# A Trainium2 decoder kernel: context tiles first in two rotary chunks, the query scale moved into a copy, and branch rows turned one branch at a time

## The reference

```
h  = norm(x)                                  # 4 tiles of 128 rows: 0,1 tokens; 2,3 context
ka, va, kc, vc, qa, qc, zb = h @ w_in          # 512 columns each (zb: 1024)
ka, qa = rope_axial(ka), rope_axial(qa)        # token tiles only
ya = differential_attention(qa * 0.125, ka, va)
yb = spatial_gate(gelu(zb))
yc = neighbourhood_attention(qc * 0.125, kc, vc)
merged = sum over b of sigmoid(h @ w_gate[b]) * (y[b] @ w_branch[b])
x  = x + gate * (merged @ w_out);  then a routed mixture of 32 experts
```

## Time and profile before

| what | value |
|---|---|
| time of three runs, us | 3181.65, 3183.58 (median), 3187.3 |
| the profiled execution, its time / its span, us | 3185.1 / 3183.4 |
| mean granted TensorE clock, share of full | 0.951 |
| PE busy | 2817.2 us, 88% of the span |
| DVE / ACT / POOL busy | 1311.8 (41%) / 930.7 (29%) / 1044.3 (33%) |
| bytes moved | 746.03 MB, mean 234 GB/s |

### The profile page before, as it was taken

One profiled execution on the slowest core, in us unless ns is written; L12 is line 12 of the kernel. 1 busy time (PEld: TensorE's weight loads), 2 busy tenths in 40 slices (PEclk: granted clock), 3 DMA queues, 4 the chain that ended last, 5 costly groups with the idle time before them and its releaser, 6 DMA issues. The chain is left out here.

```text
span 3183.4 us, 33959 instructions
## 1 busy us (share of the span) xinstructions
PE 2817.2 (88%) x13329; PEld 1876.5 (59%) x13329; DVE 1311.8 (41%) x2392; ACT 930.7 (29%) x1303; POOL 1044.3 (33%) x431
## 2 busy tenths in 40 slices
PE   7999959999998798799987999998597897999885
PEld 4777638887776486577875444443485775433331
DVE  5552123334523426763345333322527545332223
ACT  0433313335333313441212222222324332222211
POOL 0277528742875244043420000000363671000000
PEclk9999979999999899999988999999799998999998
DMA  5755675555556432222233999999242456999996
GB/s 179 265 181 177 246 280 177 181 169 179 182 186 237 161 103 81 81 92 75 100 119 142 383 421 422 422 422 402 106 137 75 146 206 273 411 422 422 422 422 266
DMA packets 208913, 746.03 MB, mean 234 GB/s; under 512 B 13877, under 2 KB 15075, under 8 KB 158833
## 3 DMA queue, kind: packets, MB, share of 16 engines
q1 hardware_dynamic: 189872, 669.61, 55.5%
q0 software_dynamic: 18880, 74.22, 6.8%
HBM read 721.00 MB, written 44.27 MB: 240 GB/s over the span
## 5 line engine op out<-in xcount | busy, mean ns | idle before, releaser
L1886 POOL TENSOR_TENSOR weight_ring_r<-weight_ring,weights_high_r 128x2048 fp32r<-128x2048 f32 x136 | 622.7, 4589 | 460.2 <-ACT weights_high_r L1495 370.0
L1495 ACT ACTIVATE weights_high_r<-weight_ring 128x2048 fp32r<-128x2048 f32 x136 | 257.1, 1901 | 654.2 <-PE banks L848 415.4
L843 PE MATMUL banks<-weights_high_r,x_transposed_r 128*128 128x512 f32 x1008 | 400.9, 398 | 32.6 <-DVE scaled_rows L2663 11.4
L2011 POOL DMA_DIRECT2D moe_y<-arena x64 | 34.1, 533 | 925.7 <-DVE arena L2711 925.7
L848 PE MATMUL banks<-weight_ring_r,x_transposed_r 128*128 128x512 f32 x1328 | 323.9, 390 | 1.0 <-POOL weight_ring_r L1886 1.0
L1886 POOL TENSOR_TENSOR weight_ring_r<-weight_ring,gates_r 128x2048 fp32r<-128x2048 f32 (+1 forms) x60 | 270.7, 4524 | 156.2 <-DVE small L2053 96.1
L848 PEld LDWEIGHTS banks<-weight_ring_r,x_transposed_r 128*128 128x128 f32 x1328 | 250.0, 188 | 53.4 <-POOL weight_ring_r L1886 1.4
L843 PEld LDWEIGHTS banks<-weights_high_r,x_transposed_r 128*128 128x128 f32 x1008 | 192.3, 191 | 77.4 <-issue 21.4
L1736 ACT ACTIVATE arena<-banks 64x1024 f32<-64x1024 f32 x64 | 65.1, 1018 | 488.8 <-PE banks L1237 488.8
L844 PE MATMUL banks<-weights_high_r,arena_r 128*128 128x512 f32 x520 | 206.7, 397 | 0.0
L2696 DVE TENSOR_TENSOR arena<-banks,arena 64x1024 f32<-64x1024 f32 x64 | 78.2, 1222 | 295.2 <-ACT arena L1736 295.2
(11 more groups left out here) (394 smaller groups left out, 4744.8 us busy)
## 6 DMA issues: line engine op xcount, KB each, us to landing
weight_ring<-in_moe_w_up SPq DMA_DIRECT2D x64, 1024.0 KB, 19.3
x_transposed<-in_moe_w_up SPq DMA_DIRECT2D x60, 1024.0 KB, 19.0
tokens_out<-in_moe_w_down SPq DMA_DIRECT2D x60, 1024.0 KB, 17.3
arena<-in_moe_w_gate SPq DMA_DIRECT2D x60, 1024.0 KB, 19.1
weight_ring<-in_moe_w_down SPq DMA_DIRECT2D x60, 1024.0 KB, 17.6
weight_ring<-in_w_in SPq DMA_DIRECT2D x56, 1024.0 KB, 5.2
weights_high<-in_moe_w_gate SPq DMA_DIRECT2D x56, 1024.0 KB, 18.7
weight_ring<-in_ffn_w_in SPq DMA_DIRECT2D x44, 1024.0 KB, 5.3
```

The costliest lines, as they stand in the source:

```text
L843: nc.tensor.matmul(banks[t][:, 0:width], xh, wh[:, k, :], start=k0 + k == 0, stop=False)
L1495: nc.scalar.activation(high(s, kn, width), slot(c, kn, width), ACT.Copy).then_inc(high_ready, 1)
L1886: nc.gpsimd.tensor_tensor(slot(c, kn, width, ring_r), slot(c, kn, width), high(s, kn, width), ALU.subtract).then_inc(low_ready, 1)
L2011: nc.gpsimd.dma_start(ys_dram[e * CAP:(e + 1) * CAP, :], A[own(e), E_Y:E_Y + D]).then_inc(ys_out[e % 2], 16)
```

## The change

Four edits. (1) `tile_order` makes PE's last (low) products, the transposes and DVE's work go through the tiles as 2, 3, 0, 1 in chunk 0 of both `g_kv` and in chunk 2 of layer 0's `g_qz`. Banks are given out in that order too. The chunk after takes them in the order 0, 1, 2, 3, so its tile 0 gets the bank of the chunk's tile 2. (2) The scale 0.125 leaves `rope_axial` and stands in the copy of the turned query rows. (3) `gate_ahead` gets a step between its two halves: PE turns the rows of the first branch there. (4) The other two branches are turned behind the gate products of n = 0 and n = 1, DVE's `parts` are split in the same way, and PE waits for one branch's copies instead of all. `src_ready` is said once.

```diff
+        def tile_order(g, n):
+            if g in g_kv and n == 0 or g is g_qz[0] and n == 2:
+                return (2, 3, 0, 1)
+            return range(g.tiles)
...
-                for t in range(g.tiles):
+                for t in order:
                     if k0 == 0:
-                        banks.append(acc_bank())
+                        banks[t] = acc_bank()
...
-                banks = [acc_bank() for _ in range(g.tiles)]
+                order = tile_order(g, 0)
+                banks = {t: acc_bank() for t in order}
...
-            def gate_ahead(g, lhs, layer):
+            def gate_ahead(g, lhs, layer, between):
...
+                between()
                 pe.wait_ge(low_back, 16 * (layer + 1))
...
-                gate_ahead(g_gate[i][0], x_late, i)
-                for t in range(tiles):
-                    for b in range(3):
-                        pe.wait_ge(src_ready, seen.next(src_ready))
-                        transposes([ar(BRANCH[b] + t * 512 + j * P, P) for j in range(4)])
-                copied()
+                branch_turned = []
+
+                def turn_branch():
+                    for t in range(tiles):
+                        transposes([ar(BRANCH[len(branch_turned)] + t * 512 + j * P, P) for j in range(4)])
+                    branch_turned.append(made.now(tr_ready))
+
+                def first_branch():
+                    pe.wait_ge(src_ready, seen.next(src_ready))
+                    turn_branch()
+                gate_ahead(g_gate[i][0], x_late, i, first_branch)
                 for n in range(6):
                     b = n % 3
                     if n > 0:
                         product(g_gate[i][n], x_late)
+                    if n < 2:
+                        turn_branch()
+                    pe.wait_ge(tr_used, branch_turned[b])
...
-                if scale == 1.0:
-                    v(tt(dst, t1, turned, ALU.add), acc_used)
-                else:
-                    v(tt(t1, t1, turned, ALU.add))
-                    v(ts(dst, t1, scale, None, ALU.mult), acc_used)
+                v(tt(dst, t1, turned, ALU.add), acc_used)
...
-                    for t in range(MAX_TILES):
+                    for t in tile_order(g_kv[layer], n):
...
-                        for t in range(tiles):
-                            copy_turned(qaT[:, :, t * P:(t + 1) * P])
+                        for t in tile_order(g_qz[layer], 2):
+                            bank = turned_bank()[:, :].rearrange("p (k c) -> p k c", k=4)
+                            v(ts(qaT[:, :, t * P:(t + 1) * P], bank, 0.125, None, ALU.mult), tr_used)
...
-                say_n = 3 * tiles
-                for _ in range(say_n):
-                    say(src_ready)
+                say(src_ready)
+
+                def branch_parts(k):
+                    for t in range(tiles):
...
+                branch_parts(0)
                 for n in range(6):
...
+                    if n < 2:
+                        branch_parts(n + 1)
```

More of the change, by code:

```diff
@@ L832, in copied, with group @@
                 pe.wait_ge(tr_used, made.now(tr_ready))
-            def group(g, lhs, banks, c, s, k0, kn, width):
+            def group(g, lhs, banks, c, s, k0, kn, width, order):
                 pe.wait_ge(high_ready, s + 1)
                 wh, wl = high(s, kn, width), slot(c, kn, width, ring_r)
-                for t in range(g.tiles):
+                for t in order:
                     if k0 == 0:
-                        banks.append(acc_bank())
+                        banks[t] = acc_bank()
                     for k in range(kn):
@@ L916, in product_chunk @@
                 col, width = g.chunks[n]
-                banks = []
+                banks = {}
                 for i, (k0, kn) in enumerate(g.groups):
                     if g.split:
-                        group(g, lhs, banks, chunk[0], g.first_split[n] + i, k0, kn, width)
+                        group(g, lhs, banks, chunk[0], g.first_split[n] + i, k0, kn, width, tile_order(g, n))
                         chunk[0] += 1
@@ L983, in turn_rows, with turn_chunk @@
                 return turned
-            def turn_chunk(tiles, wanted):
+            def turn_chunk(g, wanted):
+                tiles = g.tiles
                 def after(n, done):
                     if wanted(n):
-                        for t in range(tiles):
-                            pe.wait_ge(acc_used, done - tiles + t + 1)
+                        for place_, t in enumerate(tile_order(g, n)):
+                            pe.wait_ge(acc_used, done - tiles + place_ + 1)
                             src = hs[:, (n * tiles + t) % 4 * BANK:((n * tiles + t) % 4 + 1) * BANK]
@@ L1371, in _ @@
             turned = turn_rows(LT)
-            product(g_dil, two_split, turn_chunk(LT, lambda n: n % 6 < 4), turned, ada["dil"][3])
+            product(g_dil, two_split, turn_chunk(g_dil, lambda n: n % 6 < 4), turned, ada["dil"][3])
             dilated()
@@ L1385, in _ @@
                 entry_turned.append(turned)
-                product(g_kv[i], x_early, turn_chunk(MAX_TILES, lambda n: n in (0, 2)), turned)
-                turn_queries = turn_chunk(tiles, lambda n: n > 1)
+                product(g_kv[i], x_early, turn_chunk(g_kv[i], lambda n: n in (0, 2)), turned)
+                turn_queries = turn_chunk(g_qz[i], lambda n: n > 1)
                 def mix_and_turn(n, done):
@@ L2785, in keys_turned @@
                     if n in (1, 3):
-                        for t in range(MAX_TILES):
+                        for t in tile_order(g_kv[layer], n - 1):
                             copy_turned((kaT if n == 1 else kcT)[:, :, t * P:(t + 1) * P])
@@ L2864, in _ @@
                     if n == 3:
-                        for t in range(tiles):
-                            copy_turned(qaT[:, :, t * P:(t + 1) * P])
+                        for t in tile_order(g_qz[layer], 2):
+                            bank = turned_bank()[:, :].rearrange("p (k c) -> p k c", k=4)
+                            v(ts(qaT[:, :, t * P:(t + 1) * P], bank, 0.125, None, ALU.mult), tr_used)
                         ada_spread(g_qz[layer], 2)
-                    for t in range(tiles):
+                    for t in tile_order(g_qz[layer], n):
                         bank = product_bank()
@@ L2910, in _ @@
                         say(act_req)
-                    for t in range(tiles if n == 0 else 0):
-                        for k in range(3):
-                            dst = A_r[:, YT:YT + 6144].rearrange("p (k t c) -> p k t c", k=12, t=MAX_TILES)
-                            low = A_r[:, BRANCH[k] + t * 512:BRANCH[k] + (t + 1) * 512]
-                            parts(dst[:, k * 4:k * 4 + 4, t, :], low.rearrange("p (k c) -> p k c", k=4),
-                                  turned_bank()[:, :].rearrange("p (k c) -> p k c", k=4))
+                    if n < 2:
+                        branch_parts(n + 1)
                     if n == 0:
```

14 lines of the change are left out of this document (10 added, 4 removed).

## The result

| | before | after |
|---|---|---|
| time, us, median of four runs each | 3183.82 (3181.65 to 3187.3) | 3145.35 (3142.7 to 3147.83) |
| profiled execution, its time / its span, us | 3185.1 / 3183.4 | 3147.83 / 3146.1 |
| mean granted TensorE clock | 0.951 | 0.955 |

The account below looks back on a forecast made before the run. PE, busy 88% of the span, was taken as the bound, so its removed gaps count: 5.8 + 7.0 + 0.7 + 15.6 + 9.2 = 38.3 us, from profiled 3185.1 to 3146.8, or 3145.3 against the median; 8-in-10 range 3138 to 3155.

Parts of the forecast that it names:

- ka: Chunk behind the rotary work, one per layer: PE's wait moves before tile 3, about 3.1 us long; gain 2.9 us each.
- qa: Layer 0's query chunk: caught scaling goes, tiles reordered, high part ends earlier; gain 7.9 us, 6.2 with low clock, taken 7.0.
- Queries of layer 1: Without the scalings DVE is ready earlier, so PE's 0.59 us wait for transposes shrinks: gain 0.7 us (0 to 1).
- Gates of layer 0: Branches turned inside and behind gate products, first branch product starts without waiting at full clock: gain 15.6 us (13.5 to 16).
- Gates of layer 1: First transposes fill the 1.06 us wait; low part then waits for POOL's first subtraction: gain 9.2 us (7 to 9.5).
- Scaling in the copy: Scaling moved into the copy of turned rows costs nothing findable, bounded by 0.3 us.
- A: Rotary waits only move: last tile's wait and low clock eat half of 13.5 us at ka and qa; 3152 us, chance 0.11.
- B: POOL bounds the gate stage: one low part per layer comes a whole subtraction (4.6 us) late; 3154.5 us, chance 0.09.
- C: Nothing comes through: a later wait for a transfer takes up the whole gain; about 3182 us, chance 0.04.
- D: Clock falls repeatedly in the two gate stages, with transposes between products; 3204 us at 20% low clock, chance 0.03.
- where it goes on: Later work, including weight transfers, ACT's and POOL's parts and the expert stage, shifts with PE's groups; no term in the sum.

Follow-up runs that it names:

- the gates alone: Kernel before with only the branches turned one at a time, in the first gate product and behind it: 3160.63 us, ratio 0.9923.
- the bank with the old order: Changed kernel with the cosine product written in place into its PSUM bank, but tile order 0, 1, 2, 3 everywhere: 3136.57 us, ratio 0.9853.
- order-only run: Kernel before with the new tile order alone, no other edit: 3173.42 us, ratio 0.9965.

## Why the prediction was right or wrong

The time came out as forecast, but not every term did. Behind the first mark the stages gave 33.9 us where the sum had 38.3, and the places that the sum named gave 35.6. That the median meets the forecast to 0.1 us is luck: the interval of the gain runs from 33 to 42 us. The mechanism, two kinds of wait that go, is what the runs show.

**ka** (2.9 each). Measured 3.6 and 2.9. The picture was right, a wait of about 3.1 us that moves to the fourth tile (2.85), and so was the bracket set by the clock: the full clock held in layer 0, and fell in layer 1 behind the wait of 2.85.

**qa** (7.0). Measured 5.7, below the lower of the two values that the text gave (6.2 with a low clock). The clock was low behind the last wait (0.57), and the second sum ended some 0.4 us later than the forecast had it. I had taken a value between the two, though a gap of that length was the one for which the earlier trace rows showed the fall.

**Queries of layer 1** (0.7). Measured 0.1. The 0.59 us of the earlier trace rows went, but PE came to the first of these transposes 13.30 us after the wait for ACT's part that stands ahead of them (2379.70) instead of 12.90 (2407.99 of before): the granted clock of the 5 us behind that wait was 0.52 instead of 0.60.

**Gates of layer 0** (15.6). Measured 15.5, from the same rows: 16 transposes, 32 low-row products, 16 transposes, no wait.

**Gates of layer 1** (9.2). Measured 7.8. The run with the cosine product in its bank has the whole stage at the full clock, and there it gives 113.3 - 104.3 = 9.0. The remaining 1.2 to 1.5 are the nine products at half rate at the start of the stage: in the kernel before they ran at the full rate. There, such a fall would in part have lain in front of the 1.06 us for the low rows; that it comes through in full with that wait gone is argued from the rows, no run shows it. Nor does a run show why the clock is low there: of the twelve profiles it is low in three (the changed kernel, the gates alone, and the bank with the old order).

**Scaling in the copy** (at most 0.3 us of cost). No stage shows a cost.

**What the sum left out.** The attention stage of layer 0, whose instructions the change touches only where the turned queries are copied, became 3.1 us longer. It is not chance: the four profiles of kernels that are the same up to there (after, and the three with other turning of the branches) read 113.8, 113.8, 113.9 and 113.8, and the kernel before 110.6. It is the clock. In the kernel before, PE has the full clock from 1317 on; in the changed kernel the low stretch ahead of that place costs 1.1 us more, and a second fall behind it, with PE as busy ahead of it as before, costs 2.1. Two windows of before, then the two of the changed kernel at about the same place of the program, which there comes 11.6 us earlier:

```profile
1317.00:1327.00 10.00, 8.79 (x52) 5.40 (x52) 9.20 (x24) 5.94 (x19) 0.00 (x0) 1.00 0.00 0
1327.00:1337.00 10.00, 8.43 (x51) 5.22 (x52) 9.27 (x22) 6.02 (x20) 0.00 (x0) 1.00 0.01 2
```
```profile
1305.00:1315.00 10.00, 8.80 (x52) 5.39 (x52) 9.27 (x22) 5.96 (x19) 0.00 (x0) 1.00 0.00 0
1315.00:1325.00 10.00, 8.60 (x36) 5.69 (x38) 7.29 (x19) 4.51 (x16) 0.00 (x0) 0.66 0.00 0
```

PE does 36 instructions in the second window instead of 51, and DVE 19 instead of 22. Why the clock falls there in one kernel and not in the other stays open; no run varied that stage alone. It doesn't take the change: the gates-only run, whose program is that of before up to the end of this stage, reads 111.3, with a granted clock of 0.83 from 1328.8 to 1338.8. So the size of the fall depends on more than the instructions of the stage.

**The rivals.** A did not come: the last tile's wait was no longer than forecast. B is there in its smallest form, 0.47 us. C fell. D, that the clock falls again and again, was looked for in the wrong place and at the wrong size: the gate stage of layer 0 has a clock of 1.00, but low stretches behind qa (1.7 us), in the attention stage (3.1) and at the start of layer 1's gates (1.5) make 6.3 us. The forecast had put about half of the first into its 7.0; the rest, some 5.4 us, is more than the 4.4 us by which the stages miss the sum. The step that did not hold is the one named "where it goes on", which let all later work shift unchanged.

## What to carry to other kernels

When a DVE instruction in a row of equal ones is several times as long as the others and ends with a POOL instruction, look at where its inputs lie: with one of a sum's two inputs left in PSUM it took 0.69 us here, and this was worth more (14.6 us for three places) than putting other work in front of the wait (11 us). Change such a sum only where PE waits for it. Work for a slower engine belongs inside the last long product ahead of its need and in pieces that fit the free banks; count the places at which an edit makes somebody wait, not the kinds.

## What the runs showed of the hardware that I had not expected

- The length of a wait alone does not say whether the clock falls. Behind 2.85 us at 1106.16 the granted clock stayed at 1.00 (2.4 GHz), behind 2.85 at 1251.31 it was 0.57, a mixture with the lower level of 1.2 GHz, and the products took twice their time. At the same place as the first, in the order-only run, the granted clock behind 2.86 us was 0.70. The Trainium skill (TensorE: Matmul & The Clock Gate, Why this matters for your kernels) names gaps above about 3 us as those to avoid; the trace agrees at the first place and not at the second.
- Short waits did it too: in the run with all branches in the gate product the longest wait was 0.8 us, between groups of transposes of 0.66 us, and the clock was 0.50 from 1413 on.
- Writing a DVE product in place into a PSUM bank took 0.70 us, into SBUF 0.69.
- The same program up to the first mark took from 1022.7 to 1029.6 us. A difference of a few us between two single profiles has to be found in a stage before it is put down to an edit.
